# Down projection of a gated MLP on one core: another order of VectorE's work, and one addition moved from GpSimd to VectorE

## The reference, cut to what matters

```python
def conv_glu(h, up, conv, down):
    z = dwconv3(h @ up, conv)
    gate, val = jnp.split(z, 2, -1)
    return (jax.nn.gelu(gate, approximate=True) * val) @ down
...
    h = rmsnorm(x, norm_g[l, 2]) * (1.0 + sc2) + sh2
    y = conv_glu(h, ffn_up[l], ffn_conv[l], ffn_down[l])
    x = x + gt2 * rmsnorm(y, norm_g[l, 3])
```

## Time and profile before

| | |
|---|---|
| median of 3 runs | 2711.78 us (2710.78 to 2716.62) |
| the profiled execution | 2710.83 us |
| its span | 2708.7 us, 51619 instructions |
| granted TensorE clock, mean | 0.96 |
| TensorE (PE) busy | 2498.6 us, 92% |
| VectorE (DVE) busy | 1674.1 us, 62% |
| ScalarE (ACT) busy | 1158.1 us, 43% |
| GpSimd (POOL) busy | 1072.5 us, 40% |
| down projection, layer 0 | step 0 starts at 1597.41 us |
| down projection, layer 1 | ends with the kernel |

### The profile page before, as it was taken

How to read it: one execution, slowest core, us unless ns; L and a number is a source line. 1 busy time by engine, 2 the same in 40 slices (tenths; PEclk the granted TensorE clock), 3 DMA queues, 4 the chain that set the end, 5 groups by cost and what they waited for, 6 DMA issues and landing times. The chain is left out here.

```text
span 2708.7 us, 51619 instructions
## 1 busy us (share of the span) xinstructions
PE 2498.6 (92%) x21195; PEld 2011.0 (74%) x21195; DVE 1674.1 (62%) x2442; ACT 1158.1 (43%) x1886; POOL 1072.5 (40%) x725
## 2 busy tenths in 40 slices
PE   5998989898999989979999999986988999999998
PEld 4776656566888876768888878765776888887876
DVE  7775722464666637656656676956565666667686
ACT  5211342464555534444444344454344443444443
POOL 2301122211222202237887853331323878884333
PEclk8999999898999989989999999997998999999999
DMA  7686534712222124223433355222222333335423
GB/s 243 212 278 218 187 124 171 251 32 70 76 74 78 54 73 148 71 82 105 132 109 117 108 198 172 63 101 88 85 80 74 112 126 125 103 123 195 159 70 124
DMA packets 301964, 339.45 MB, mean 125 GB/s; under 512 B 29055, under 2 KB 207988, under 8 KB 301732
## 3 DMA queue, kind: packets, MB, share of 16 engines
q1 hardware_dynamic: 292092, 329.83, 37.4%
q10 hardware_dynamic: 9640, 6.33, 0.8%
HBM read 253.23 MB, written 82.88 MB: 124 GB/s over the span
## 5 line engine op out<-in xcount | busy, mean ns | idle before, releaser
L3337 POOL TENSOR_TENSOR cg_u_lo<-cg_u_raw,cg_u_hi 128x512 fp32r<-128x512 f32 x210 | 316.8, 1516 | 143.7 <-ACT cg_u_hi L3162 143.7
L131 PE MATMUL cg_ps<-m_hi,cg_u_hi 128*128 128x512 f32 x768 | 300.8, 392 | 21.5 <-DVE cg_u_lo L3479 21.5
L3162 ACT ACTIVATE cg_u_hi<-cg_u_raw 128x512 fp32r<-128x512 f32 x216 | 132.1, 629 | 394.7 <-PE cg_ps L133 232.0
L132 PE MATMUL cg_ps<-m_lo,cg_u_hi 128*128 128x512 f32 x768 | 300.2, 391 | 0.0
L133 PE MATMUL cg_ps<-m_hi,cg_u_lo 128*128 128x512 f32 x768 | 300.2, 391 | 0.0
L131 PE MATMUL cg_ps<-over_y_tx,cg_u_hi 128*128 128x512 f32 x480 | 186.7, 389 | 0.0
L133 PE MATMUL cg_ps<-over_y_tx,cg_u_lo 128*128 128x512 f32 x480 | 186.7, 389 | 0.0
L132 PE MATMUL cg_ps<-over_y_tx,cg_u_hi 128*128 128x512 f32 x480 | 186.7, 389 | 0.0
L131 PEld LDWEIGHTS cg_ps<-m_hi,cg_u_hi 128*128 128x128 f32 x768 | 145.2, 189 | 52.6 <-DVE cg_u_lo L3479 22.3
L3414 DVE SCALAR_TENSOR_TENSOR cg_z<-cg_ps,top_conv_f,cg_z 128x1023 f32<-128x1023 f32 x88 | 112.9, 1283 | 93.8 <-ACT cg_z L3187 93.8
L132 PEld LDWEIGHTS cg_ps<-m_lo,cg_u_hi 128*128 128x128 f32 x768 | 145.2, 189 | 30.3
(11 more groups left out here) (522 smaller groups left out, 6436.4 us busy)
## 6 DMA issues: line engine op xcount, KB each, us to landing
cg_u_raw<-in_ffn_up SPq DMA_DIRECT2D x88, 512.0 KB, 5.4
qkv_mw<-in_ada_w SPq DMA_DIRECT2D x12, 2048.0 KB
scr_act<-cg_z SPq DMA_DIRECT2D x44, 512.0 KB, 2.6
raw_over_h_b<-in_ffn_down SPq DMA_DIRECT2D x56, 256.0 KB, 2.9
cg_u_raw<-scr_act SPq DMA_DIRECT2D x44, 256.0 KB, 4.5
cg_u_raw<-scr_asum SPq DMA_DIRECT2D x44, 256.0 KB, 2.6
scr_asum<-cg_over_split_sums SPq DMA_DIRECT2D x42, 256.0 KB, 2.3
qkv_mw<-in_ada_w SPq DMA_DIRECT2D x8, 1024.0 KB, 11.3
```

The costliest lines, as they stand in the source:

```text
L131: nc.tensor.matmul(out, a_hi, b_hi, start=first, stop=False)
L132: nc.tensor.matmul(out, a_hi, b_lo, start=False, stop=False)
L3162: A(u_hi[:, n % RING], source(g, i), ACT.Copy).then_inc(uhi_done, 1)
L3337: G.tensor_tensor(u_lo[:, n % RING], source(g, i), u_hi[:, n % RING].bitcast(F32), ALU.subtract).then_inc(ulo_done, 1)
```

## The change

`EARLY` = 50 replaces the literal 46. The parts are:

1. The low parts of steps 0, 1 and 2 stand earlier on VectorE, in the last group of the up projection, and those of steps 3 and 4 stand right behind that group's last convolution, ahead of `product`. ScalarE's splits of steps 3 and 4 stand ahead of the last `gelu`.
2. `second_sum(k)` is at n = k + 5 (before, at n = k, the first three ahead of step 3), `fourth_sum(k)` at n = k + 16 (before k + 11).
3. VectorE takes three combinations from PSUM (L3544, L3548, L3568) ahead of the weight sum of the same step, or a step earlier.
4. The A22T4 low parts of b are at n = 50 to 60 (before 46 to 56).
5. `add_x` of the tail's first four tiles is VectorE's, right behind `scale_y`; GpSimd no longer has it.

SP's program is not changed.

```diff
+EARLY = 50
...
-        B_ORDER = [n for m in range(SPLITS) for n in ([m] if m < LAST else []) + ([LAST + m - 46] if 46 <= m < 46 + KD else [])]
+        B_ORDER = [n for m in range(SPLITS) for n in ([m] if m < LAST else []) + ([LAST + m - EARLY] if EARLY <= m < EARLY + KD else [])]
...
+            for j in (3, 4):
+                split_down_a(j)
+                split_down_b(j)
             gelu(NG - 1)
-            for n in range(3, SPLITS):
+            for n in range(5, SPLITS):
...
-            for n in range(S2T2 * KD, SPLITS):
-                if n < LAST:
-                    low_weights(n)
-                for t, at in enumerate(TAIL_AT):
-                    if n == at + 1:
-                        tail.add_x(pool, G, t, y[:, t, :])
+            for n in range(S2T2 * KD, LAST):
+                low_weights(n)
...
-                if t >= HT:
-                    dve.wait_ge(tail.x_done, t)
-                    tail.add_x(dve, V, t, y[:, t, :])
+                tail.add_x(dve, V, t, y[:, t, :])
...
+                    if g == NG - 1:
+                        low_down_a(0)
+                        low_down_b(0)
...
                     if g == NG - 1:
-                        for j in range(2):
-                            low_down_a(j)
-                            low_down_b(j)
+                        low_down_a(1)
+                        low_down_b(1)
...
+            for j in (3, 4):
+                low_down_a(j)
+                low_down_b(j)
             product(NG - 1)
             activation_sum(NG - 1)
-            for k in range(3):
-                second_sum(k)
-            for n in range(3, SPLITS):
+            for n in range(5, SPLITS):
...
-                if n < KD:
-                    second_sum(n)
-                elif n < 2 * KD:
-                    fourth_sum(n - KD)
-                elif S4B22 * KD <= n < S4B22 * KD + KD:
-                    second_weight_sum(n - S4B22 * KD)
+                if 5 <= n < 5 + KD:
+                    second_sum(n - 5)
+                if 16 <= n < 16 + KD:
+                    fourth_sum(n - 16)
                 if n == S4B22 * KD + 1:
...
+                if S4B22 * KD <= n < S4B22 * KD + KD:
+                    second_weight_sum(n - S4B22 * KD)
-                if n == S3T3 * KD + 1:
+                if n == S3T3 * KD:
...
-                if 46 <= n < 46 + KD:
-                    low_down_b(LAST + n - 46)
+                if EARLY <= n < EARLY + KD:
+                    low_down_b(LAST + n - EARLY)
...
-                if n == LAST + 1:
+                if n == LAST:
```

More of the change, by code:

```diff
@@ L3299, in _ @@
                     split_down_b(n)
-                if 46 <= n < 46 + KD:
-                    split_down_b(LAST + n - 46)
+                if EARLY <= n < EARLY + KD:
+                    split_down_b(LAST + n - EARLY)
                 if n % KD == 1 and n // KD in (1, 2):
```

## The result

The changed kernel takes **2760.5 us** (median of 4 runs, 2756.8 to 2762.9), the kernel before 2714.2 us beside it (4 runs): a ratio of 1.0178, interval 1.0160 to 1.0195. It is slower, by more than the 2751 us that the prediction gave, and inside its range. The profiled execution took 2762.9 us for a span of 2760.9 us.

What follows compares the result with a forecast made beforehand. TensorE, busy 92% of the span, bounds the kernel, so only its waits matter. Layer 0: 22.0 - 3.0 + 3.0 - 4.5; layer 1: 22.0 - 3.0 + 4.0 - 0.5; together +40.0 on 2710.8, 2751 us, range 2735 to 2765.

Steps and rivals of the forecast that it cites:

- Bound, and part 1: TensorE's waits set the time; early low parts remove the down projections' pause at step 3, 7.2 us per layer.
- the ring: Steps 11 to 21: SP's block load waits for second_sum, which waits for earlier blocks; 5.34 us per turn against 2.72 per step.
- the landing in the turn: Landing of the 256 KB weight block after SP's order, steps 11 to 21: taken as 2.9 us, median of 11.
- Step 11: Down projection, layer 0: it waits for ScalarE's copy of product 0 from PSUM, starting at 1634.0, 7.1 us late.
- Item 1 of that list: Layer 0: step 7 ends at 1618.8; two ScalarE splits, two low parts and second_sum(5) follow, until 1621.3.
- Clock behind step 21: The last gap leaves TensorE at 1.2 GHz for some matmuls behind step 21: +1.5 us.
- Parts 3 and 4: Earlier PSUM sums and later A22T4 low parts shrink the waits at steps 33 and 55: -3.0 us per layer.
- Part 5 and what is pushed back: Steps 57 to 60: VectorE has three more low parts and one add_x: +3 us in layer 0, +4 in layer 1.
- The tail of layer 0: GpSimd no longer delays low parts behind add_x and tail chains get shorter: -4.5 us in layer 0, 0 in layer 1.
- Loads land late: Rival, chance 0.12: every turn's load lands in 3.9 us, 1.0 more, +21 us in all, 2772 us.
- The ring is not closed: Rival, chance 0.05: the weight block is ordered in time, so only gains stay, -18 us, 2693 us.
- The low clock did not linger: Rival, chance 0.05: TensorE stays at 1.2 GHz for three steps behind step 21, +14 us, 2765 us.

Runs made afterwards that it cites:

- three and four steps later: The changed kernel with second_sum and fourth_sum three, or four, steps later than before instead of five: 2688.7 us (ratio 0.9911) and 2695.3 us (ratio 0.9939).
- blocks ordered in time: The changed kernel, sums still five steps later, with SP ordering A12B21's weight block of step k at j = k, not k + 5: 2692.1 us, ratio 0.9929.
- part 2 alone: The kernel before with only second_sum(k) moved to n = k + 5 and fourth_sum(k) to n = k + 16: 2773.0 us, ratio 1.0233.
- part 1 alone: The kernel before with the early low parts and splits of steps 0 to 4, and the sums three steps later: 2695.7 us, ratio 0.9945.
- part 5 alone: The kernel before with only add_x of the tail's first four tiles moved from GpSimd to VectorE: 2703.9 us, ratio 0.9973.

## Why the prediction was right, and where it was short

- **Bound, and part 1.** Right. The pause at step 3 is gone, with the low clock behind it: -7.0 and -7.6 us at step 4, counted from step 0. The forecast 7.2 has 0.4 in it for an earlier step 0, which that count leaves out.
- **Part 2, the ring.** Right in its mechanism: three kernels that open it, from VectorE's side (three and four steps later) and from SP's (blocks ordered in time), all end below the kernel before, and part 2 alone makes it.
- **The mis-sized term is the landing in the turn**, 2.9 us. Order to split took 3.35 on the mean, so nine turns took 52.0 us (low part of b, 1641.09 to 1693.04) and not 48.1: +3.9 in layer 0, and +2.7 in layer 1 (2537.16 to 2587.87, order to split 3.25 on the mean). The rest of the turn was right, 2.4 us. About half of the error was in the reading of the earlier trace rows. Ten of those eleven loads carry a landing, of 2.79 to 3.89 us: median 2.9, mean 3.1. A ring adds its turns up, so its price is the mean and not the median. My reason for the low end, that one pair of loads per turn leaves the queues emptier, was wrong too: the queues were emptier (DMA engines busy for 0.28 of the time against 0.61 around those ten loads), and the loads were no faster. Why they took another 0.1 to 0.2 us was not tested. The Trainium skill ("DMA: Bandwidth & Descriptors", the anatomy of one DMA) makes it 2.6 us, an estimate from its figures for GpSimd's path; the trace does not agree for these loads of SP.
- **A term left out.** The forecast took the start of VectorE's low part of step 21 for TensorE's step 21. TensorE began 0.84 us behind it in both layers (1693.04, 1693.88).
- **Step 11**: 7.1 us late by its due time was forecast, 9.0 measured. Item 1 of that list failed: it had ScalarE's splits of steps 9 and 10 ready, and they waited for activation loads. ScalarE's splits, VectorE's first sum and SP's three loads behind it:

```profile
1623.39 0.63 ACT L3215 ACTIVATE cg_a<-cg_u_raw 128x512 fp32r<-128x512 f32 x1 [2.58 <-DMA cg_u_raw<-scr_act]
1626.85 0.63 ACT L3215 ACTIVATE cg_a<-cg_u_raw 128x512 fp32r<-128x512 f32 x1 [2.30 <-DMA cg_u_raw<-scr_act]
...
1628.72 0.69 DVE L3448 TENSOR_TENSOR y_x<-y_x,cg_u_raw 128x512 f32<-128x512 f32 x1
...
1629.48 0.32 SPq L3077 DMA_DIRECT2D cg_u_raw<-scr_act  x1
1629.85 0.43 SPq L3052 DMA_DIRECT2D y_y<-scr_asum  x1
1630.32 0.43 SPq L3126 DMA_DIRECT2D raw_over_h_b<-in_ffn_down  x1
```

  The sum ends 26.6 us behind step 0 (1602.77); the forecast had 24.3. The two loads that followed took 3.70 and 3.55 us for 3.8, as forecast. The low part of step 12 then started 1.2 and 1.1 us later than forecast. With the turns (3.9 and 2.7) and the 0.84 these make 5.9 and 4.6 of the 6.5 and 4.6 us by which step 21 came later than the +20.5 of the text. The 0.6 left in layer 0 is in the base, mostly the 0.4 of step 0.
- **Clock behind step 21.** +1.5 was taken. In layer 0 it did not come: step 21 ran at 2.4 GHz. In layer 1 step 21 took 4.4 us for 2.7. The wait at step 33 shrank by 0.4 and 0.5 us, so from step 21 to step 33 layer 0 gained 0.3 and layer 1 lost 1.1.
- **Parts 3 and 4.** -3.0 per layer forecast, -3.0 and -3.0 between steps 33 and 55.
- **Part 5 and what is pushed back.** +3 and +4 forecast, +3.3 and +4.2 between steps 55 and 61. The tail of layer 0: -4.5 forecast, -5.5 measured; layer 1 0 forecast, -0.4. These terms, and the -3.0 above, were picks between wide bounds (0 and -4.5, 0 and +6, 0 and -12), so that they came out so near is in part luck.
- **Sum.** Forecast +17.5 and +22.5, measured +21.4 and +26.9. Of the 8.3 us between them, step 21 makes 11.1; the clock behind it gave back 2.2 and the tail 1.4. Steps 55 to 61 cost 0.4 more, and the 0.5 that the forecast took off for layer 1's dearer pause was in its step 21 already. The remaining 1 us of the distance from 2751 to 2760.5 is less than the runs of one kernel scatter by.
- **The rivals.** "Loads land late" had the right direction and half the size: 0.45 us a turn for 1.0. "The ring is not closed" named 2693 us, which is what the kernels measured in which it is open (2688.7 and 2692.1). The low clock did not linger.

## What to carry to other kernels

A wait in an in-order queue delays everything behind it, so moving one cheap operation later moves all loads that stand behind the wait for it. If a load behind the wait feeds the engine that ends the wait, there is a ring: add up one turn from order to order, and divide by the steps that the order runs ahead. While the turn is shorter than that many steps, it is free; beyond, it sets the pace of the whole stage, and the largest wait of the stage may be only where the pace shows first. A turn is paid many times, so take the mean of its loads, not their median. Order loads that need nothing ahead of waits that they don't need.

## What the runs showed of the hardware

The granted clock behind waits of the same length differed. Windows of the first 3 us or so of steps 15 to 20 of layer 0 (columns: window, its length, busy time of PE, PEld, DVE, ACT, POOL with counts, granted clock, DMA share, GB/s):

```profile
1659.18:1662.00 2.82, 2.82 (x12) 2.14 (x12) 1.06 (x2) 0.00 (x0) 0.00 (x0) 1.00 0.31 94
1665.07:1668.50 3.43, 3.43 (x9) 2.77 (x10) 2.13 (x2) 0.00 (x0) 1.58 (x1) 0.57 0.49 130
1670.94:1674.00 3.06, 2.96 (x12) 2.15 (x12) 1.06 (x2) 0.00 (x0) 0.00 (x0) 1.00 0.31 90
1677.45:1681.00 3.55, 3.55 (x10) 2.83 (x11) 2.14 (x2) 0.00 (x0) 1.59 (x1) 0.61 0.45 141
1683.24:1686.50 3.26, 2.98 (x12) 2.14 (x12) 1.05 (x2) 0.00 (x0) 0.00 (x0) 1.00 0.53 159
1688.63:1692.00 3.37, 3.37 (x8) 2.69 (x9) 2.14 (x2) 0.00 (x0) 1.59 (x1) 0.52 0.43 156
```

Step 15, behind a wait of 2.85 us, runs at 2.4 GHz (1.00 granted). Step 16, behind 2.88, has its first six matmuls at 1.2 GHz (1665.63 and 1666.06, 0.43 apart; 0.57 granted over the window). Steps 17 and 19, behind 1.52 and 1.22 us, are high; 18 and 20, behind 3.54 and 2.41, are low for eight and seven matmuls, step 18 only from its fourth on. In layer 1 the steps do not take turns: step 17 is high behind 2.54 us, step 15 low behind 2.55.

The same step in other executions shows it better. Step 55 of the kernel before, behind a wait of 1.96 us in layer 0 and of 1.93 in layer 1:

```profile
1758.16:1760.90 2.74, 2.74 (x12) 2.29 (x13) 2.74 (x5) 0.00 (x0) 0.57 (x1) 1.00 0.60 191
...
2634.79:2638.00 3.21, 3.21 (x8) 2.52 (x9) 3.21 (x6) 0.00 (x0) 0.61 (x1) 0.54 0.46 163
```

The step took 2.82 us in the first and 4.41 in the second. With part 1 alone it was the other way round (4.40 and 2.82), and with part 5 alone both were low. So a wait of 2 to 3 us may or may not cost 1.6 us of low clock behind it, and a single trace cannot tell whether a change made the difference.

The Trainium skill ("TensorE: Matmul & The Clock Gate", on loop structure) says: "long DMA wait between every matmul → PE goes cold". The prediction took the rule without the word "long". The longest wait here agrees: behind the 8.84 us at step 11 all twelve matmuls ran 0.43 apart or more, 5.25 us in all. Behind the shorter ones steps 16, 18 and 20 went low and steps 15, 17 and 19 did not. The low clock cost nothing in the ring: behind steps 16, 18 and 20 TensorE still waited, for 1.52, 1.22 and 0.74 us.

The other thing that I had not expected is the landing: loads of 256 KB, issued in pairs with nothing else near them in the queue, took 2.9 to 4.1 us until the split started (2.8 to 3.8 in layer 1), with the DMA engines busy for 0.28 of the time:

```profile
1640.00:1694.00 54.00, 36.62 (x121) 27.35 (x122) 22.45 (x29) 14.03 (x26) 7.98 (x5) 0.84 0.28 88
```
